# Moving the rankings of a decoder step between the merges, the query and a dense product stage

## The reference

```python
q = einsum('td,dhpk->thpk', hb, w_peer_query)        # 8 heads x 2 halves, width 128
s = einsum('thpk,hpnk->thpn', q, peer_sub_keys)      # 16 score rows of 128 keys per token
s1, i1 = top_k(s[:, :, 0], 16); s2, i2 = top_k(s[:, :, 1], 16)
cand = s1[..., :, None] + s2[..., None, :]           # 256 pairs per head
top, sel = top_k(cand, 16); w = softmax(top)         # 16 experts of 16384 per head
act = gelu(einsum('thkd,td->thk', peer_u[idx], hb))
out = einsum('thk,thkd->td', w * act, peer_v[idx])   # x += out, then a last RMSNorm
```

## Time and profile before

| | us |
|---|---|
| runs shown: median (lowest to highest, 3 runs) | 5396.97 (5388.49 to 5401.4) |
| profiled execution | 5362.92 |
| its span | 5361.1 |
| busy PE (matmul) | 4029.9 (75%) |
| busy DVE | 2772.7 (52%) |
| busy ACT (ScalarE) | 391.5 (7%) |
| busy POOL (GpSimd) | 1366.4 (25%) |

### The profile page before, as it was taken

How to read it: one execution, slowest core, us unless ns; L and a number is a source line. 1 busy time by engine, 2 the same in 40 slices (tenths; PEclk the granted TensorE clock), 3 DMA queues, 4 the chain that set the end, 5 groups by cost and what they waited for, 6 DMA issues and landing times.

```text
span 5361.1 us, 38323 instructions
## 1 busy us (share of the span) xinstructions
PE 4029.9 (75%) x14110; PEld 2429.6 (45%) x14110; DVE 2772.7 (52%) x3563; ACT 391.5 (7%) x822; POOL 1366.4 (25%) x1241
## 2 busy tenths in 40 slices
PE   7999688888779999999999796999999990000000
PEld 5887445554229984755555443544443430000000
DVE  1001732222110001587767666786765447799998
ACT  1000321222010000000000001000000000000000
POOL 0000000001430000124445443112222117777533
PEclk8999888778779999999999898999999995555555
DMA  3221141101446664668999987499999989999999
GB/s 138 76 70 63 52 151 67 35 23 39 147 127 243 241 233 149 241 264 362 413 406 414 409 338 284 185 364 397 388 403 419 357 326 344 344 400 409 416 422 381
DMA packets 234186, 1413.00 MB, mean 264 GB/s; under 512 B 34704, under 2 KB 35536, under 8 KB 86416
## 3 DMA queue, kind: packets, MB, share of 16 engines
q0 software_dynamic: 138960, 916.70, 43.1%
q1 hardware_dynamic: 81984, 458.79, 22.9%
q10 hardware_dynamic: 13088, 35.50, 1.7%
HBM read 1385.08 MB, written 25.75 MB: 263 GB/s over the span
## 4 chain that ended last, share of the span: by engine, by line
PE 53%; DMA 19%; DVE 11%; issue 8%; POOL 7%; ACT 2%; ACTq 0%; DVEq 0%; POOLq 0%
PE psum L811 15%; PE psum L542 10%; DMA arena<-in_v,arena 10%; PE psum L939 9%; DMA arena<-in_u_cols 7%; POOL arena L504 3%; PE psum L920 3%; DVE psum L1775 3%; POOL arena L522 2%; PE psum L850 2%; POOL arena L472 1%; PE psum L873 1%; PE psum L730 1%; DVE arena L1653 1%; PE psum L714 1%
## 5 line engine op out<-in xcount | busy, mean ns | idle before, releaser
L811 PE MATMUL psum<-arena 128*128 128x160 f32 (+1 forms) x5120 | 1175.7, 393 | 4.1 <-DVE arena L1508 3.3
L1775 DVE SCALAR_TENSOR_TENSOR psum<-arena,psum 128x2048 f32<-128x2048 f32 x381 | 897.3, 2355 | 193.4 <-DMA arena<-in_v,arena 178.0
L811 PEld LDWEIGHTS psum<-arena 128*128 128x128 f32 x5120 | 835.6, 190 | 343.7 <-issue 4.1
L939 PE MATMUL psum<-arena 128*128 128x512 f32 x2048 | 915.2, 600 | 32.2 <-DMA arena<-in_u_cols 26.9
L504 POOL DMA_INDIRECT arena<-in_v,arena x544 | 611.6, 1124 | 926.7 <-DVE arena L1653 371.4
L504 POOL DMA_INDIRECT arena<-in_u,arena x288 | 380.9, 1323 | 1440.0 <-DVE arena L1596 629.8
L542 PE MATMUL psum<-arena 128*128 128x272 f32 x2432 | 579.8, 402 | 80.7 <-ACT arena L1027 44.3
L939 PEld LDWEIGHTS psum<-arena 128*128 128x128 f32 x2048 | 378.7, 190 | 568.1 <-issue 419.1
L542 PEld LDWEIGHTS psum<-arena 128*128 128x128 f32 x2432 | 472.0, 195 | 185.3 <-issue 75.6
L1752 DVE CUSTOM_DVE_ANT_0 arena<-arena,psum 128x2048 f32<-128x2048 f32 x128 | 290.5, 2286 | 146.7 <-DMA arena<-in_u,arena 146.4
L465 POOL COPY stage_idx<-pages 128x16 uint32 x8 | 1.5, 194 | 1423.3 <-PE psum L700 1290.8
(11 more groups left out here) (267 smaller groups left out, 2950.0 us busy)
## 6 DMA issues: line engine op xcount, KB each, us to landing
arena<-in_w_merge SPq DMA_DIRECT2D x160, 1024.0 KB, 5.1
arena<-in_u_cols SPq DMA_DIRECT2D x256, 512.0 KB, 10.2
arena<-in_w_out SPq DMA_DIRECT2D x32, 1024.0 KB, 4.9
arena<-in_w_query SPq DMA_DIRECT2D x32, 1024.0 KB, 4.8
arena<-in_w_proj SPq DMA_DIRECT2D x31, 1024.0 KB, 4.8
products<-arena ACTq DMA_DIRECT2D x32, 512.0 KB, 12.3
arena<-in_v,arena POOLq DMA_INDIRECT x544, 11.1
arena<-in_w_mem_k SPq DMA_DIRECT2D x8, 1024.0 KB, 4.8
```

Of the source, the lines that this page charges most:

```text
L811: last = mm(out, w[:, (off + k) * P:(off + k + 1) * P], src[:, k0 + k, lo:hi], start=(k == 0), stop=(k == n - 1))
L939: last = mm(psum[:, 4 + DENSE * (b % 2) + t, :], hfT_b[:, k0 + k, t * P:(t + 1) * P], u_tiles[n % 4][:, k, :], start=(k0 + k == 0), stop=( ...
L1775: V.scalar_tensor_tensor(a, four(row), atmp_b[:, t, r:r + 1], a if r else four(x1_b[:, t, :]), ALU.mult, ALU.add).then_inc(s("rows_used"), 1)
```

## The change: where rankings and rows stand

1. Samples' rankings: in pieces of 6, 5 and 5 (merges 16 to 19), not four blocks of four in one merge; the sample tile's four pairs pieces stand one per merge in M = 20 to 23.
2. Rows: first pieces of 4, 4, 4 (5, 5, 6 before); 15 per merge from M = 18; in M = 31 the last four stand behind `merge_out(31)`. Six rows among the norms go; the three behind them stay. The query takes two rows per step, so v4 ends with the query; it is summed in SBUF (`acc_s`), and ScalarE's copy in b == 5 goes.
3. Dense tiles' scores: PE writes those of tiles 0 and 1 to other PSUM banks, ScalarE copies them to SBUF (`kept_scores`), and DVE ranks them later, four in a piece, among rows 15 to 50 of u2. In the query DVE ranks tile 2 alone. The first product waits for the last copy.
4. Pairs pieces: three of tile 2 behind u2 rows 3, 7 and 11, the eight of tiles 0 and 1 every five rows from row 55.
5. `HELD` is 72, not 40. ScalarE's places change: M == 24, 25, 28 and b == 17, 21. The last norms of tiles 3 and 4 stand 32 rows later in v2.
6. Buffers are moved to other places of the arena.

```diff
-HELD = 40
+HELD = 72
@@ PE, query of the B tiles
                     if q >= 2:
                         pe.wait_ge(s("ranked"), 16 + q - 1)
+                        pe.wait_ge(s("scores_kept"), 16 + 2 * (q - 1))
                     for t in B_TILES:
-                        last = mm(psum[:, 2 + q % 2, t * P:(t + 1) * P], ...)
+                        last = mm(psum[:, (4 if t < 2 else 2) + q % 2, t * P:(t + 1) * P], ...)
@@ PE, dense products
+                    elif k0 == 0 and t == 0:
+                        pe.wait_ge(s("scores_kept"), 16 + 32)
...
-            pe.wait_ge(s("sample_kept"), 1)
+            pe.wait_ge(s("x1_done"), 2)
@@ ScalarE
-                if M == 20:
+                if M == 24:
                     act.wait_ge(s("top_shifted"), 1)
...
-                if M == 27:
+                if M == 25:
                     gelu_tanh(0, atmp_3)
-                if M == 30:
+                if M == 28:
                     gelu_tanh(1, atmp_s)
@@ ScalarE, query of the B tiles
+                if u >= 1:
+                    act.wait_ge(s("scored"), 16 + u)
+                    for t in range(2):
+                        a_(kept_scores(t, u - 1), psum[:, 4 + (u - 1) % 2, t * P:(t + 1) * P], ACT.Copy).then_inc(s("scores_kept"), 1)
@@ ScalarE, dense products
-                if b == 5:
-                    act.wait_ge(s("x1_done"), 2)
-                    a_(four(acc_s), acc[0], ACT.Copy).then_inc(s("sample_kept"), 1)
-                if b == 20:
+                if b == 17:
                     act.wait_ge(s("top_shifted"), 2)
...
-                if b == 25:
+                if b == 21:
                     gelu_tanh(2, atmp_b[:, 2, :])
@@ DVE, merges
+            for M in range(18, 32):
+                if M == 25:
                     share_tops(w_a, tsum_a, 0, s("w_a_ready"))
...
                 take(4)
                 merge_out(M - 1)
+                if M in (18, 19):
+                    rank_samples(5 * M - 84, 5 * M - 79)
+                if 20 <= M < 24:
+                    pairs_a(4, 2 * (M - 20))
...
                 take(7)
                 products_in(M)
-                take(4)
+                if M < 31:
+                    take(4)
             merge_out(31)
+            take(4)
@@ DVE, take(n)
+                    elif c >= first_row["v", 4]:
...
+                        w = atmp_s[:, r:r + 1]
+                        if r == 0:
+                            dve.sem_inc(s("x1_done"), 1)
+                            ins = V.tensor_scalar(acc_s, row, w, None, ALU.mult)
+                        else:
+                            ins = V.scalar_tensor_tensor(acc_s, row, w, acc_s, ALU.mult, ALU.add)
@@ DVE, norms and query
                 norm_scale("ffn", t, 2 + t)
-                take(2)
...
-            take(2)
+            take(3)
+            dve.wait_ge(s("spread"), 64 + 64 + 64)
+            gelu_out(1, atmp_s, acts_s, w_s)
+            dve.wait_ge(s("hfT_stored"), 8 + 12)
+            def rank_b(t, u, scores):
+                best16(scores, v16_b[:, t, u, :], is_b[:, t, :], sc2_b)
+                return V.tensor_copy(i16_b[:, t, u, :], is_b[:, t, :])
             for u in range(16):
                 dve.wait_ge(s("scored"), 16 + u + 1)
-                for t in B_TILES:
-                    best16(psum[:, 2 + u % 2, t * P:(t + 1) * P], ...)
+                rank_b(2, u, psum[:, 2 + u % 2, 2 * P:3 * P]).then_inc(s("ranked"), 1)
                 dve.wait_ge(s("ranked"), 16 + u + 1)
-                take(1)
+                take(2)
@@ DVE, u2
-                if r % 8 == 7 and r < 64:
-                    pairs_b(r // 32, 2 * (r // 8 % 4))
-                if r == 64:
+                if r in (3, 7, 11):
+                    pairs_b(2, (r + 1) // 2)
+                if 12 <= r < 52 and r % 5 == 0:
+                    for n in range(4 * (r // 5 - 3), 4 * (r // 5 - 3) + 4):
+                        do(rank_b(n // 16, n % 16, kept_scores(n // 16, n % 16)))
+                if 52 <= r < 92 and r % 5 == 0:
+                    pairs_b((r // 5 - 11) // 4, 2 * ((r // 5 - 11) % 4))
+                if r == 92:
                     shift_tops(w_b, tsum_b)
```

More of the change, by code:

```diff
@@ L312, in build, with kept_scores @@
         qT_b = region(BK + D, 2, B_N)
-        cand_b, eq_b = region(F1 + 256, 2, 256), region(F1 + 256 + 2048, 2 * TOPK, TOPK)
-        v16_b, i16_b = region(F1 + 256 + 4096, 3, 16, 16), region(F1 + 256 + 4096 + 768, 3, 16, 16)
-        assert F1 + 256 + 4096 + 2 * 768 <= F1 + KD * B_N and BK + D + 2 * B_N <= F1 + 256
+        cand_b, eq_b = region(F1 + 256, 2, 256), region(F1 + 768, 2 * TOPK, TOPK)
+        v16_b, i16_b = region(F1 + 1280, 3, 16, 16), region(F1 + 2048, 3, 16, 16)
+        kept = region(F1 + 2816, 26, P)
+        kept_rest = region(BK + 512, 6, P)
+        assert F1 + 2816 + 26 * P == F1 + KD * B_N and BK + D + 2 * B_N <= F1 + 256
+        def kept_scores(t, u):
+            n = 16 * t + u
+            return kept[:, n, :] if n < 26 else kept_rest[:, n - 26, :]
         BX = 3 * D
@@ L926, in _ @@
                         pe.wait_ge(s("ranked"), 16 + q - 1)
+                        pe.wait_ge(s("scores_kept"), 16 + 2 * (q - 1))
                     for t in B_TILES:
-                        last = mm(psum[:, 2 + q % 2, t * P:(t + 1) * P], qT_b[:, q % 2, t * P:(t + 1) * P], keysT_b[:, q, :], start=True, stop=True)
+                        last = mm(psum[:, (4 if t < 2 else 2) + q % 2, t * P:(t + 1) * P], qT_b[:, q % 2, t * P:(t + 1) * P], keysT_b[:, q, :], start=True, stop=True)
                     last.then_inc(s("scored"), 1)
@@ L1646, in take @@
                         V.tensor_tensor_reduce(row, row, lone_s, 1.0, 0.0, ALU.mult, ALU.add, acts_s[:, r:r + 1]).then_inc(s("rows_used"), 1)
+                    elif c >= first_row["v", 4]:
+                        r = c - first_row["v", 4]
+                        row, landed, k = place(c)
+                        dve.wait_ge(landed, k)
+                        w = atmp_s[:, r:r + 1]
[4 more added lines that the diff above has]
+                            ins = V.scalar_tensor_tensor(acc_s, row, w, acc_s, ALU.mult, ALU.add)
+                        ins.then_inc(s("rows_used"), 1)
+                        dve.wait_ge(s("rows_used"), c + 1)
                     else:
```

78 lines of the change are left out of this document (24 added, 54 removed).

## The result

Seven timed runs of each kernel, side by side: the changed kernel took 5367.99 us in the median (5355.36 to 5377.29), the old one 5393.08 (5379.99 to 5405.53). The ratio is 0.9946, 95% interval 0.9931 to 0.9961: about 0.5% faster. The forecast was 5330, the range 5295 to 5374. The sign and the range held, the size did not: 25 us were won where 67 were promised.

What follows compares the result with a forecast made beforehand. Four stages each had their own limit: PE in merges and query, PE beside a full DMA in the products, then one chain behind the release. Terms -7 - 10 - 0 - 10 - 40 = -67 us gave 5330 us, range 5295 to 5374.

Steps and rivals of the forecast that it cites:

- Merges: B merges: DVE's 51 to 52 us fit beside PE's 51.6, the 3.35 us stall goes, w_out starts earlier; -7 us.
- Rival 2: B merges: DVE falls behind and PE pays the excess in stalls; -49 us in all, 5348 us; chance 0.11.
- Norms: Behind w_out: six rows no longer stand between DVE's norms, so scaling starts after the first root; -10 us.
- Query: Query steps: one ranking and two rows take DVE 7.3 us, under 10.99, and ScalarE's score copies stay hidden; 0 us.
- Products: First product to release: PE's 2048 records take 936 us, not 945, with fewer rows gathered freely; -10 us.
- rival 1: Products: gathers run free for all 201 rows, so PE's stage ends 23 us later; -34 in all, 5363; chance 0.11.
- Rival 3: Products: a late u2 end delays ScalarE's tanh and the copies behind it; slower, 5410 us; chance 0.05.
- Held rows: Release to v2's end: 32 more rows issued ahead, 183 issues at 1.284 us remain, 235 us for 276.1; -40 us.
- Rival 4: Release to v2's end: the time goes by rows, 3.17 us each, -101 for -40; 5269 us; chance 0.05.
- Port: v4 summed in SBUF: 32 gather issues in the query lengthened by up to one DVE row each, at no cost.
- Carried over: Old kernel's median 5396.97 was 34 us above its profiled execution; that difference was added to 5296, giving 5330 us.
- unfavourable ends: Worst case of each term, summed as +11 - 8 + 10 - 30, about -17 us, for the range's upper end.

Runs made afterwards that it cites:

- twelve rows: Changed kernel with 12 gathered rows, not 15, per merge in M = 18 to 23, the 18 rows moved behind the norms and into the query; 5318.85 us, ratio 0.9862.
- fourteen rows: Changed kernel with 14 rows, not 15, beside each piece in merges 18 to 23, six moved to the query; ratio 0.9956, with weights computed earlier 0.9929.

## Why the prediction was right in sign and wrong in size

**Merges: the failed step.** I wrote: "51 to 52 us, next to PE's 51.6", and from it that the 3.35 us stall goes "and no other comes": -7 us. That was the sum of DVE's work, with rows at 2.3 to 2.4 us as if each lay ready. It was said for intervals that took 58 to 61. The rows do not lie ready: beside 15 of them the DMA engines need 50.7 of 51.6 us, and the four buffers cannot carry it over a pause of 12.7. My argument for it, that the last ten merges had kept pace with 15 rows, was true and did not cover the case, since they have no piece. I had even written that the DMA is full from 2450 on the earlier trace rows and looked only for room before that, for the number of rows, not for their pace. Rival 2 named the place (11 in 100), by DVE's work and at 18 us above the forecast; it was 52.5, and by landings. Against before it is 45.5: 27.4 us more of stalls (30.72 for 3.35), 13.2 in slower merges (839.3 us busy for 826.1) and 5.0 in the gap ahead of `w_out` (33.51 for 28.54). The twelve rows show the term right for a kernel that leaves the DMA its slack: -6.5.

**Norms: right.** -10.0; PE waits 42.81 us for the scaled rows, 52.39 before.

**Query: right in the steps, wrong at the end.** Steps of 10.99 us. The first product waits 7.44 us for its columns, since GpSimd issues the last v4 gathers at 3496 to 3510 and they share the DMA with the first tiles of `u_cols`. I had allowed 2. The kernel that takes them earlier shows nearly two thirds of it. The prediction priced the copies of the scores here, not these loads.

**Products: -8.6 for -10.** The last product ends 936.7 us behind the start of the first, 936 were forecast. The rate of PE under free gathers is 206 records per 100 us (205 in the earlier trace rows). u2 ended 618.5 us behind the first product where +621 was counted (the ranking cycles, 5 x 2.3 and 10.3, are 21.8 us and not 22.3, which would give +617). DVE's wait at the tanh was 11.50 us and not 22 because the tanh came sooner: the 22nd product copy ended at +631.2, 28.7 us a step, not at +643. GpSimd had 58 us at the hold to spare. But the -10 is the net of two larger terms, as HELD = 40 shows: -23.6 from the rest of the change, and +15 from the 32 held rows. So rival 1, the free stream, has its mechanism confirmed and its size not: it takes back 15 of 24. In the old kernel with HELD = 72, where gathers run free to the last product, the stage is 6.7 us longer, not the 23 of its end. Rival 3 needed u2 to end 90 us later and is out.

**Held rows: right.** 234.5 us where 235 were forecast, and back to 276.0 with HELD = 40: the stretch goes by issues, 1.28 us each. Rival 4 (by rows) is out. What I did not see is the condition: it holds only while the held rows can be issued before the release, and rows issued up to the end put the release itself off by 7 us. The old kernel with 72 wins nothing.

**Port.** The summing of v4 in the query shows what the prediction's paragraph on it said. GpSimd's timeline and DVE's, in one query step of the changed kernel:

```profile
3441.35 2.39 POOL L512 DMA_INDIRECT arena<-in_v,arena  x1 [7.36 <-DVE arena L1668]
3444.05 0.94 POOL L512 DMA_INDIRECT arena<-in_v,arena  x1 [0.30 <-issue]
```

```profile
3438.19 4.74 DVE L1668 SCALAR_TENSOR_TENSOR arena<-arena,newmask 128x2048 f32<-128x2048 f32 x2
```

The issue that falls into DVE's second row lasts to 3443.7, past that row's end at 3442.9; the one behind it takes 0.94. The Trainium skill, "SBUF — State Buffer", section "Who interferes with whom", has it that a DVE instruction with two inputs in SBUF contends with a GpSimd instruction that reads SBUF. The trace agrees: 2.39 against 0.94 us. In the query this cost nothing. In the merges it has a part in the hole: behind a piece the refills beside DVE's four rows took 2.21, 1.91 and 1.91 us, and the fourth, beside none, 0.94. How much of the 9 us it makes was not tried.

**Carried over.** From the first merge on, the two traces differ by 6 us in the changed kernel's favour, the timings by 25. The profiled execution of before is 30 us under its median, and 11 us of that could lie ahead of the first merge; the other 19 are put down to it too, which is an inference. For it: other kernels stand in the same way to that trace (twelve rows: 52 us under it by marks, 74 by the ratio; HELD = 40: 40 above it by marks, 18 by the ratio). Against it: for the old kernel with HELD = 72 marks and ratio differ by 5 us only. Had I compared with that trace as it stands, the forecast would have been 5296; carrying over its distance to the median brought it nearer.

**The range.** The measured median lies 6 us inside its upper end, and that is partly luck. The sum of the unfavourable ends takes +10 for the products where the text gives +23, and leaves out the +2 of the query; with them it is about -2, or 5395. And the end for the merges was +11 where +45.5 came: the range held because the other stages came out near the forecast.

## What to carry to other kernels

Beside a stream that fills the DMA engines, count the bytes per step of the other engine (here one merge of PE) before adding work: 50.7 of 51.6 us is no slack, and then a pause of the consumer that is longer than its buffers last is paid. A sum of an engine's busy times says nothing of this; look for an interval of the trace that has both the rate and the pause, and if there is none, price it by the worse. And a hold (work allowed ahead of a release) is worth its issues only up to the point that the queue reaches by the release; past it, it costs. What it lets run also slows the stage beside it and the store that the release waits for: 15 and 7 us here.

## What the runs showed of the hardware

- Holes: with four 1.05 MB gathers on the way, a consumer's pause of 12.7 us empties all 16 DMA engines for about 9 us, and GpSimd stands 14.88 us; afterwards DVE gets a row every 3.4 us beside the weight stream.
- The clock: stalls of PE of 3 to 8 us, one in 60 us, went with a granted clock of 0.93 to 0.98 in the windows and 160 records in 53.4 to 54.8 us, where 51.6 is the value at 1.00. So a stall cost up to 3 us more than its length. Stalls of 0.60 and 2.12 us, with fourteen rows, were followed by 160 records in 51.84.
- A DMA share of 1.0 is not one rate: 372 and 409 GB/s for the same order of instructions in two executions, and 407 and 373 within one.
- A 512 KB store from SBUF to DRAM landed in 2.7 us while GpSimd issued nothing, and in 10.0 to 10.2 us beside 1.05 MB gathers that filled the DMA engines.
- Single traces of one code differ by 28 us ahead of the first B merge (2191.8 and 2220.3, both of the changed kernel's variants).
